# Hybrid decoder step: squares summed by PE, row scaling on two engines, norm weight in the split

## What is computed

```python
def _rmsnorm(x, w):
    xf = x.astype(F32)
    y = xf * lax.rsqrt(jnp.mean(xf * xf, axis=-1, keepdims=True) + EPS)
    return (y * w.astype(F32)).astype(x.dtype)

hn = _rmsnorm(x, norm_w)
u = hn @ w_in
z_ssd, xbc, dt_raw, q, k, v, z_att, g_ssd, g_att = jnp.split(u, _split_points(), axis=-1)
```

## Time and profile before

| | us |
|---|---|
| median of 3 runs | 1071.72 (1069.91 to 1073.2) |
| the profiled execution's own time | 1071.67 |
| its span on the core | 1069.9 |
| PE busy | 998.1 (93%) |
| DVE busy | 714.5 (67%) |
| ACT busy | 534.0 (50%) |
| POOL busy | 270.4 (25%) |

### The profile page before, as it was taken

One profiled execution on the slowest core, in us unless ns is written; L12 is line 12 of the kernel. 1 busy time (PEld: TensorE's weight loads), 2 busy tenths in 40 slices (PEclk: granted clock), 3 DMA queues, 4 the chain that ended last, 5 costly groups with the idle time before them and its releaser, 6 DMA issues.

```text
span 1069.9 us, 21735 instructions
## 1 busy us (share of the span) xinstructions
PE 998.1 (93%) x8420; PEld 934.2 (87%) x8420; DVE 714.5 (67%) x1135; ACT 534.0 (50%) x1289; POOL 270.4 (25%) x339
## 2 busy tenths in 40 slices
PE   3998889999999998999999999999999987799998
PEld 2998878999999886399988988988999987799998
DVE  6857577576777387677878878888845577634332
ACT  5435556566574655045555555555545658212110
POOL 0222122242332111011321321421314898100000
PEclk9999999999999999999999999999999999799999
DMA  9361533345541257563463643543679997422221
GB/s 385 122 244 62 240 124 139 142 190 222 197 159 61 82 189 257 175 236 129 175 239 131 231 181 130 232 180 124 239 281 371 369 346 255 165 80 79 105 84 50
DMA packets 30261, 198.00 MB, mean 185 GB/s; under 512 B 4520, under 2 KB 6792, under 8 KB 20688
## 3 DMA queue, kind: packets, MB, share of 16 engines
q1 hardware_dynamic: 25664, 183.09, 45.1%
q0 software_dynamic: 4496, 13.54, 3.3%
HBM read 179.89 MB, written 104.70 MB: 266 GB/s over the span
## 4 chain that ended last, share of the span: by engine, by line
PE 63%; DVE 14%; ACT 10%; issue 7%; DMA 4%; POOL 1%; SPq 0%; ACTq 0%; DVEq 0%; POOLq 0%
PE bank L698 30%; PE bank L732 14%; PE bank L745 5%; DVE cacc L1715 4%; ACT wH L1283 3%; PE bank L921 1%; DMA slot<-in_state_ssm 1%; DVE yL L2146 1%; PE bank L821 1%; PE bank L861 1%; DMA out_tail<-tail 1%; PE bank L878 1%; PE bank L780 1%; PE bank L998 1%; DVE hst L2070 1%
## 5 line engine op out<-in xcount | busy, mean ns | idle before, releaser
L698 PE MATMUL bank<-xH,wH 128*128 128x260 f32 x976 | 204.2, 290 | 4.4 <-DVEq L1629 1.8
L698 PE MATMUL bank<-xH,wL 128*128 128x260 f32 x976 | 197.1, 283 | 0.0
L698 PE MATMUL bank<-xL,wH 128*128 128x260 f32 x976 | 196.5, 283 | 0.0
L1283 ACT CAST wH<-w_raw 128x2048 fp32r<-128x2048 f32 (+1 forms) x81 | 122.1, 1507 | 91.3 <-PE bank L698 83.5
L698 PEld LDWEIGHTS bank<-xH,wH 128*128 128x128 f32 x976 | 150.7, 189 | 14.6 <-issue 12.3
L698 PEld LDWEIGHTS bank<-xH,wL 128*128 128x128 f32 x976 | 150.9, 189 | 0.0
L698 PEld LDWEIGHTS bank<-xL,wH 128*128 128x128 f32 x976 | 150.8, 189 | 0.0
L732 PE MATMUL bank<-wH,xH 128*128 128x256 f32 x480 | 142.8, 298 | 7.7 <-DVE xL L1663 7.0
L732 PE MATMUL bank<-wL,xH 128*128 128x256 f32 x480 | 137.7, 287 | 0.0
L732 PE MATMUL bank<-wH,xL 128*128 128x256 f32 x480 | 137.3, 286 | 0.0
L1684 DVE TENSOR_TENSOR wL<-w_raw,wH 128x2048 fp32r<-128x2048 f32 (+1 forms) x45 | 104.7, 2327 | 48.0 <-ACT wH L1283 46.9
(11 more groups left out here) (298 smaller groups left out, 2122.4 us busy)
## 6 DMA issues: line engine op xcount, KB each, us to landing
w_raw<-in_weights SPq DMA_DIRECT2D x62, 1024.0 KB, 5.2
out_kvs<-in_cache SPq DMA_DIRECT2D x16, 2044.0 KB, 10.8
ring<-in_cache SPq DMA_DIRECT2D x48, 256.0 KB, 3.8
slot<-in_state_ssm SPq DMA_DIRECT2D x16, 512.0 KB, 6.3
out_ssm_s<-slot POOLq DMA_DIRECT2D x16, 512.0 KB, 5.7
out_kvs<-in_cache SPq DMA_DIRECT2D x8, 508.0 KB, 7.2
out_kvp<-st POOLq DMA_DIRECT2D x18, 128.0 KB, 3.7
out_kvp<-vv POOLq DMA_DIRECT2D x18, 128.0 KB, 2.1
```

Source lines behind the costliest of these rows:

```text
L698: mm = pe.matmul(bk[hf].tile[:, 0:HALF], wslot(w, i)[:, k, s * P:(s + 1) * P], x[:, k, hf * HALF:(hf + 1) * HALF], start=(k == 0 and n == ...
L1283: return nc.scalar.copy(out, in_)
```

## The change

- The list begins ("squares"), ("init"), ("split", 0), ("xparts"): the first split of weights stands behind the row scale on ACT and DVE, and the split of x is a step of its own. SP issues its DMAs in the same order as before.
- DVE adds only tiles 0 to 3 into tile 0 and tile 5 into tile 4. PE multiplies ones with four tiles (0, 4, 6, 7) for each half, accumulating in PSUM: 8 matmuls in place of 2, 16 passes in place of 4.
- The tiles are scaled by `rs` alone: the four even ones by DVE, the four odd ones by POOL, each a product of two 128x520 tiles.
- The norm's weight is a per-partition factor in ACT's cast to `xH` and in DVE's subtraction to `xL`.
- Two semaphores of a late step ("sampleparts") are made one; the order of work there is the same.

```diff
-    out = [("squares",), ("split", 0), ("init",)]
+    out = [("squares",), ("init",), ("split", 0), ("xparts",)]
 PE:
                     pe.wait_ge(S["constants_set"], 2)
-                    pe.wait_ge(S["squares_added"], 1)
                     for hf in range(2):
                         banks[hf].take(pe, ("ms", hf))
-                        pe.matmul(banks[hf].tile[:, 0:HALF], ones[:, :], xsq[:, 0, hf * HALF:(hf + 1) * HALF],
-                                  start=True, stop=True).then_inc(banks[hf].filled, 1)
+                    for k, what, n in ((0, "squares_added", 1), (4, "squares_added", 2), (6, "rows_squared", 7), (7, "rows_squared", 8)):
+                        pe.wait_ge(S[what], n)
+                        for hf in range(2):
+                            mm = pe.matmul(banks[hf].tile[:, 0:HALF], ones[:, :], xsq[:, k, hf * HALF:(hf + 1) * HALF],
+                                           start=(k == 0), stop=(k == 7))
+                            if k == 7:
+                                mm.then_inc(banks[hf].filled, 1)
 SP:
+                elif op == "squares":
+                    load(0)
+                    sp.dma_start(par[:, :], params).then_inc(S["tables_loaded"], 16)
                 elif op == "init":
-                    sp.dma_start(par[:, :], params).then_inc(S["tables_loaded"], 16)
                     sp.dma_start(con[:, :], consts).then_inc(S["tables_loaded"], 16)
-                elif op in ("split", "load"):
+                elif op == "load" or op == "split" and a[0] > 0:
 POOL:
+                elif op == "init":
+                    pool.wait_ge(S["row_scale_ready"], 1)
+                    for k in range(1, KD, 2):
+                        nc.gpsimd.tensor_tensor(xw[:, k, :], xw[:, k, :], rs[:, :], ALU.mult).then_inc(S["scaled_odd_ready"], 1)
 ACT:
+                elif op == "xparts":
+                    act.wait_ge(S["tables_loaded"], 32)
                     for k in range(KD):
-                        act.wait_ge(S["scaled_rows_ready"], k + 1)
-                        cp(xH[:, k, :], xw[:, k, :]).then_inc(S["x_high_ready"], 1)
+                        act.wait_ge(S[("scaled_rows_ready", "scaled_odd_ready")[k % 2]], k // 2 + 1)
+                        A(xH[:, k, :], xw[:, k, :], ACT.Copy, scale=par[:, PW_NORM + k:PW_NORM + k + 1]).then_inc(S["x_high_ready"], 1)
 DVE:
                 elif op == "squares":
-                    for k in range(1, KD):
+                    for k, into, last in ((1, 0, False), (2, 0, False), (3, 0, True), (5, 4, True)):
                         dve.wait_ge(S["rows_squared"], k + 1)
-                        ins = TT(xsq[:, 0, :], xsq[:, 0, :], xsq[:, k, :], ALU.add)
+                        ins = TT(xsq[:, into, :], xsq[:, into, :], xsq[:, k, :], ALU.add)
...
                 elif op == "init":
+                    dve.wait_ge(S["row_scale_ready"], 1)
+                    for k in range(0, KD, 2):
+                        TT(xw[:, k, :], xw[:, k, :], rs[:, :], ALU.mult).then_inc(S["scaled_rows_ready"], 1)
+                elif op == "xparts":
                     dve.wait_ge(S["tables_loaded"], 32)
-                    dve.wait_ge(S["row_scale_ready"], 1)
-
-                    for k in range(KD + 2):
-                        if k < KD:
-                            STT(out=xw[:, k, :], in0=xw[:, k, :], scalar=par[:, PW_NORM + k:PW_NORM + k + 1], in1=rs[:, :],
-                                op0=ALU.mult, op1=ALU.mult).then_inc(S["scaled_rows_ready"], 1)
-                        if k >= 2:
-                            dve.wait_ge(S["x_high_ready"], k - 1)
-                            TT(xL[:, k - 2, :], xw[:, k - 2, :], xH[:, k - 2, :].bitcast(F32), ALU.subtract).then_inc(S["x_low_ready"], 1)
+                    for k in range(KD):
+                        dve.wait_ge(S["x_high_ready"], k + 1)
+                        STT(out=xL[:, k, :], in0=xw[:, k, :], scalar=par[:, PW_NORM + k:PW_NORM + k + 1], in1=xH[:, k, :].bitcast(F32),
+                            op0=ALU.mult, op1=ALU.subtract).then_inc(S["x_low_ready"], 1)
```

More of the change, by code:

```diff
@@ L571, in hybrid_kernel @@
             sample_q_ready sample_squares_ready sample_state_read
-            sample_outer_ready sample_scale_ready sample_state_ready sample_xdt_ready sample_y_high_ready sample_y_low_ready sample_y_ready scaled_c_ready scaled_rows_ready
+            sample_outer_ready sample_scale_ready sample_state_ready sample_xdt_ready sample_y_parts_ready sample_y_ready scaled_c_ready scaled_rows_ready scaled_odd_ready
             selectors_loaded state_stored0 state_stored1
@@ L692, in proj_cols @@
                             if k == 0:
-                                pe.wait_ge(S["sample_y_low_ready"], 1)
+                                pe.wait_ge(S["sample_y_parts_ready"], 2)
                         if kind == "wo" and j == 0 and s == 0:
@@ L1612, in _ @@
                     act.wait_ge(S["sample_y_ready"], 1)
-                    cp(yH[:, :, 0:B], ygn[:, :, 0:B]).then_inc(S["sample_y_high_ready"], 1)
+                    cp(yH[:, :, 0:B], ygn[:, :, 0:B]).then_inc(S["sample_y_parts_ready"], 1)
                 elif op == "mix":
@@ L1646, in _ @@
                 elif op == "squares":
-                    for k in range(1, KD):
+                    for k, into, last in ((1, 0, False), (2, 0, False), (3, 0, True), (5, 4, True)):
                         dve.wait_ge(S["rows_squared"], k + 1)
-                        ins = TT(xsq[:, 0, :], xsq[:, 0, :], xsq[:, k, :], ALU.add)
-                        if k < KD - 1:
+                        ins = TT(xsq[:, into, :], xsq[:, into, :], xsq[:, k, :], ALU.add)
+                        if last:
+                            ins.then_inc(S["squares_added"], 1)
+                        else:
                             ch.link(ins)
-                    ins.then_inc(S["squares_added"], 1)
                 elif op == "init":
+                    dve.wait_ge(S["row_scale_ready"], 1)
+                    for k in range(0, KD, 2):
+                        TT(xw[:, k, :], xw[:, k, :], rs[:, :], ALU.mult).then_inc(S["scaled_rows_ready"], 1)
+                elif op == "xparts":
                     dve.wait_ge(S["tables_loaded"], 32)
-                    dve.wait_ge(S["row_scale_ready"], 1)
-                    for k in range(KD + 2):
-                        if k < KD:
-                            STT(out=xw[:, k, :], in0=xw[:, k, :], scalar=par[:, PW_NORM + k:PW_NORM + k + 1], in1=rs[:, :],
-                                op0=ALU.mult, op1=ALU.mult).then_inc(S["scaled_rows_ready"], 1)
-                        if k >= 2:
-                            dve.wait_ge(S["x_high_ready"], k - 1)
-                            TT(xL[:, k - 2, :], xw[:, k - 2, :], xH[:, k - 2, :].bitcast(F32), ALU.subtract).then_inc(S["x_low_ready"], 1)
+                    for k in range(KD):
+                        dve.wait_ge(S["x_high_ready"], k + 1)
+                        STT(out=xL[:, k, :], in0=xw[:, k, :], scalar=par[:, PW_NORM + k:PW_NORM + k + 1], in1=xH[:, k, :].bitcast(F32),
+                            op0=ALU.mult, op1=ALU.subtract).then_inc(S["x_low_ready"], 1)
                 elif op == "rope":
@@ L2147, in _ @@
                 elif op == "sampleparts":
-                    dve.wait_ge(S["sample_y_high_ready"], 1)
-                    TT(yL[:, :, 0:B], ygn[:, :, 0:B], yH[:, :, 0:B].bitcast(F32), ALU.subtract).then_inc(S["sample_y_low_ready"], 1)
+                    dve.wait_ge(S["sample_y_parts_ready"], 1)
+                    TT(yL[:, :, 0:B], ygn[:, :, 0:B], yH[:, :, 0:B].bitcast(F32), ALU.subtract).then_inc(S["sample_y_parts_ready"], 1)
                 elif op == "mix":
```

## The result

The changed kernel takes 1078.58 us (median of 8 runs, 1075.88 to 1079.99) against 1072.2 for the kernel before (median of 8 runs too; the 1071.72 above is of three of them). The two medians are 6.4 us apart. Its profiled execution took 1077.12 us with a span of 1075.0, against 1071.67 and 1069.9. Two further measurements of the same kernel gave 1.0048 (1.0029 to 1.0067) and 1.0032 (1.0014 to 1.0049).

The account below looks back on a forecast made before the run. PE was taken to bound the kernel, delayed by a later start: x's split ending 3.2 us later, less 0.86 slack, costs PE 2.35. So 1071.67 + 2.35 = 1074.0 us, range 1069.6 to 1076.3.

Parts of the forecast that it names:

- the start of PE's passes: Sum of squares on PE: first four passes from 7.75 us, twelve more from 9.8, ending with the drain at 13.8.
- R: End of the Exp that makes the row scale: forecast 15.3 us against 15.91 before, between 14.9 and 16.55.
- the slack at PE: Wait for a bank DVE frees, near 40 us: 0.86 us in hand, taken off DVE's 3.2 us lateness.
- so no more is added: Beyond 60 us: DVE has slack and waits for PE again, so the loss of 2.35 us stays as it is.
- The turns between DVE and POOL: Scaling of x: the engines exclude each other, each POOL tile ending 1.16 us later and each DVE tile 0.57.
- E - R: Time from R to E, the end of the last subtraction to `xL`: forecast 14.66 us against 10.84 before.
- Rival (a): Scaling: DVE and POOL exclude each other little or not, E 1.1 us earlier, total 1069.7 us; chance 0.12.
- The moved split: First weight split behind the row scale: DVE's 2.29 us `wL` stands on the path, giving back what DVE is spared.
- The weight in the casts: ACT's eight casts with the weight, 0.64 us each, end well ahead of DVE; DVE's subtractions take 0.67 each.
- Rival (b): PE's squares: all sixteen passes stay at the low clock, R = 16.55, total 1075.3 us; chance 0.17.
- rival (c): PE waits for DVE's rows earlier or once more, all of E's 3.2 us reach the end: 1075.0 us; chance 0.11.
- Rival (d): Sum of squares: DVE's adds were never late, so nothing is gained at R; inside R's range, no separate chance.

Follow-up runs that it names:

- a_psum: Changed kernel with DVE reading the row scale from two PSUM banks, in halves of 260 columns; ratio 1.003 to the kernel before.
- a_nopool: Changed kernel with all eight scalings on DVE and none on POOL; ratio 1.0003 to the kernel before.
- only_weight: Kernel before with only the norm's weight moved into the casts to xH and xL; ratio 1.0002 to the kernel before.
- b_again: Kernel before, unaltered, measured and traced a second time; ratio 1.0008 to the kernel before.
- b_delay5: Kernel before with five needless 128x520 additions on DVE between row scale and first scaling; ratio 1.0028 to the kernel before.
- b_pesquares: Kernel before with only the sum of squares shared with PE (four tiles, sixteen passes); ratio 0.9981 to the kernel before.
- q_threes: b_pesquares with PE working on the first three rows tile by tile and k's tables formed later; ratio 0.9999 to the kernel before.
- a_dvesquares: Changed kernel with the old sum of squares (seven adds on DVE, four passes on PE); ratio 1.0021 to the kernel before.

## Why the prediction was wrong

The sign was right and 2.35 us was forecast; 5.2 were measured, and the time of 1078.6 lies above the range. The steps that failed are the start of PE's passes, which made R 0.7 too early, the slack at PE, read as 0.86 where it was 0.42, and "so no more is added" for everything behind 62 us. By its steps:

- **The turns between DVE and POOL** held. E - R was to be 14.66 and is 14.49. Rival (a), that they run side by side, is refuted by the 1.78 us products, and a_psum shows the condition. The alternation was read from rows around 521 and 910 us, so this is no luck.
- **The moved split** held: 1.72 us by a_nopool against only_weight, part of it hidden before by the wait for R.
- **The weight in the casts** costs nothing, as costed (E - R 10.85 in only_weight, 10.84 before).
- **R was 0.7 too early**: 15.3 forecast, 15.80, 16.00 and 16.28 found. The term that was mis-sized is the start of PE's passes, 7.75 in my sum and 8.3 to 9.0 in the traces. I took the landing of the fourth x tile from one trace (its squaring began at 6.2) as fixed; in the changed kernel it began at 6.7, 7.0 and 7.4. Before, nothing hung on it, since the first Ln stood behind ACT's cast and that behind the landing of the weights; so R was 15.91, 15.76 and 15.79 (before, b_again, b_delay5) with that squaring at 6.2, 6.5 and 6.8. Taking that cover away put the landing of x on the path. Rival (b), passes at the low clock throughout, didn't happen in the changed kernel: their distance falls from 0.43 to 0.22 at 13.2, 4.2 us after their start, and they end at 14.8 for the late start. It was not far off, however. In the eight traces with these passes they took 5.1 to 6.8 us, as the distance halved 2.8 us (b_pesquares) to 6.1 us (q_threes) after the first; in q_threes that is rival (b) but for the last two passes. The 6.05 of the forecast, 7.75 to 13.8, is met by the 5.72, 5.82 and 6.19 of the changed kernel's traces.
- **The slack was 0.42, not 0.86.** The prediction read it at the bank of the third row. Nearer is the transpose of the row before, L768, which needs ACT's copy `qT` (39.04 + 0.36 = 39.40 before, while the transpose began at 40.04), and in the changed kernel the wait is that one (0.56 us, at 43.63, which is 0.20 behind the end of the copy). So 0.64 - 0.20 = 0.44 was in hand, and PE is 0.41 or 0.42 less late than E in all three traces. E's 3.76 in the mean therefore cost 3.3 at PE: rival (c)'s mechanism in part, the slack half as large.
- The sum with the measured terms: 2.35 + 0.7 (R) - 0.2 (E - R) + 0.4 (slack) = 3.3, which is what the traces show at 62 us. The rest, to 5.2 in the first measurement and to some 4.6 over three, lies behind 62 us, where the prediction put the term at nothing with only the stretch from 60 to 100 us looked at. The three traces drift by 1.5, 6.9 and 1.1 us there, in the turns and the low clock shown above; b_delay5's ratio speaks against a growth of the delay as such, and whether the change itself adds anything there stays open.
- **The base and the spread.** The forecast of 1074.0 stands on 1071.67. The kernel before had a median of 1072.2 in eight runs and of 1074.1 to 1074.3 in the 29 to 35 runs on other chips of the experiments. A spread of 1.1 for measurement and forecast together was too small for kernels whose medians scatter by 0.1 to 0.2%; part of the miss in the time is this, and not the change.
- **Rival (d)**, that nothing is gained at R, held. By a_dvesquares the old sum gives R = 14.6 in the new order, 1.3 earlier than before by the order alone; PE's share of the squares, a loss of 0.9 to 1.2, and the later landings used this up.

## What to carry to other kernels

Here POOL could relieve DVE only where DVE's instructions, those behind the shared work too, had at most one operand in SBUF. Before handing it half of a loop, look in the trace for two such instructions side by side, and read how much longer each takes. Before moving work from under a wait, ask what else that wait was hiding: here a landing of x, a copy on ACT and 1.7 us of weight split. And read a landing, and the moment at which the clock rises, from several traces, since their scatter is of the size of such a gain.

## What the runs showed of the hardware

- Two DVE and POOL instructions with two operands in SBUF each take turns, one whole instruction at a time, seven turns in a row: 0.70 becomes 1.78 on DVE, 1.29 becomes 1.74 on POOL. With DVE's second operand in PSUM neither is longer (0.75 for two halves of 260 columns beside POOL, 0.76 before POOL starts; 1.29 for POOL beside DVE). I hadn't expected the condition to be so sharp.
- TensorE's clock rose during the passes and fell again while PE waited for x, so that the rows began at the low level. How long PE had worked on the passes when the clock rose differed from trace to trace, from 2.8 to 6.1 us. Windows of the changed kernel (length, busy us and count by engine, granted clock, DMA share, GB/s):

```profile
13.20:20.00 6.80, 1.59 (x8) 1.03 (x6) 3.69 (x3) 5.31 (x8) 3.64 (x3) 1.00 1.05 448
20.00:30.20 10.20, 3.98 (x18) 4.01 (x19) 10.20 (x11) 4.24 (x6) 3.25 (x2) 0.50 0.53 206
30.20:36.00 5.80, 5.77 (x48) 5.57 (x47) 4.92 (x11) 1.27 (x4) 0.00 (x0) 1.00 0.44 181
```
